# A second score row taken behind the next turns, three of ten slabs copied by VectorE, later traffic held until k is in

## What is computed

```python
def attend(q, k, v, scale):
    # query head h uses kv head h // (Hq/Hk), 128 queries at a time
    sc = jnp.einsum("bqhgd,bkhd->bhgqk", qi, k) * scale
    p = jax.nn.softmax(sc, axis=-1)
    return jnp.einsum("bhgqk,bkhe->bqhge", p, v)

o1 = attend(dq[:, :, :, 0], dk[:, :, :, 0], dv, sc)      # differential: 4 pairs of heads, values of 128
o2 = attend(dq[:, :, :, 1], dk[:, :, :, 1], dv, sc)
o_diff = rmsnorm(o1 - lam * o2, subln_g) * (1.0 - lam_init)
o_gqa = attend(gq, gk, gv, sc)                           # grouped: 8 query heads, 2 kv heads, values of 64
```

## Time and profile before

| | |
|---|---|
| time, median of 3 runs | 2223.13 us (2220.74 to 2223.78) |
| profiled execution: time, span | 2224.07 us, 2222.0 us |
| TensorE: products, weight loads | 1999.5 us (90%), 1490.4 us (67%) |
| VectorE, ScalarE, POOL | 1546.1 us (70%), 1378.3 us (62%), 938.0 us (42%) |
| mean granted clock of TensorE | 0.961 of full |
| first score row, last store of attention | 396.66 us, 929.06 us |
| a copy of a turned slab by ScalarE, L907 | 0.60 us, 240 of them |
| reduction of a score row, L940; softmax row, L900 | 1.49 us, 128 of them; 1.33 us, 128 of them |

### The profile page before, as it was taken

How to read it: one execution, slowest core, us unless ns; L and a number is a source line. 1 busy time by engine, 2 the same in 40 slices (tenths; PEclk the granted TensorE clock), 3 DMA queues, 4 the chain that set the end, 5 groups by cost and what they waited for, 6 DMA issues and landing times.

```text
span 2222.0 us, 36247 instructions
## 1 busy us (share of the span) xinstructions
PE 1999.5 (90%) x9592; PEld 1490.4 (67%) x9592; DVE 1546.1 (70%) x2158; ACT 1378.3 (62%) x2000; POOL 938.0 (42%) x869
## 2 busy tenths in 40 slices
PE   5899995688988889879989999999999999999993
PEld 2776664555555555467646888888877888888881
DVE  3752373585336743246446999999988999999995
ACT  2422121465656566522336999899878998999982
POOL 1010011651115511006453666656665666666663
PEclk7999998799999999888999999999999999999997
DMA  7464345711122121248536999799999977789967
GB/s 260 138 185 134 108 133 175 215 39 41 36 53 44 29 44 36 81 160 157 131 90 251 307 352 315 230 297 300 353 330 351 347 241 224 229 245 353 303 152 255
DMA packets 162651, 429.16 MB, mean 193 GB/s; under 512 B 26993, under 2 KB 82033, under 8 KB 137889
## 3 DMA queue, kind: packets, MB, share of 16 engines
q1 hardware_dynamic: 92818, 294.36, 36.6%
q0 software_dynamic: 60048, 116.89, 23.6%
q10 hardware_dynamic: 9712, 16.99, 2.6%
HBM read 360.83 MB, written 96.26 MB: 206 GB/s over the span
## 4 chain that ended last, share of the span: by engine, by line
PE 45%; DMA 6%; DVE 2%; issue 2%; ACT 1%; SPq 1%; ACTq 0%; POOL 0%; DVEq 0%; POOLq 0%
PE ps_d L2031 11%; PE ps_r L2014 8%; PE ps_r L2016 7%; PE ps_r L2015 7%; DMA w_experts<-in_w_exp_down 5%; PE ps_y L1937 4%; PE ps_y L2004 3%; PE ps_g L1954 2%; PE ps_d L1971 1%; PE ps_g L2038 1%; PE ps_t L1917 0%; DMA y_tiles_odd<-y_scratch 0%; DMA o_in<-o_scratch 0%; DVE x_row L1672 0%; DMA y_scratch<-e_y,e_target_index 0%
## 5 line engine op out<-in xcount | busy, mean ns | idle before, releaser
L1782 DVE TENSOR_TENSOR w_gate_up_low<-w_experts,w_gate_up_high 128x1024 fp32r<-128x1024 f32 x416 | 489.2, 1217 | 18.5 <-ACT w_gate_up_high L1551 18.4
L1551 ACT ACTIVATE w_gate_up_high<-w_experts 128x1024 fp32r x416 | 416.5, 1049 | 31.9 <-SPq L1309 16.9
L940 DVE TENSOR_REDUCE neg_max<-ps_scores 128x1 f32<-128x1280 f32 x128 | 190.2, 1489 | 232.9 <-PE ps_scores L1025 232.5
L2014 PE MATMUL ps_r<-w_gate_up_high,gatheredT_high 128*128 128x512 f32 x832 | 336.0, 404 | 3.0 <-DVE gatheredT_low L1788 2.7
L1440 POOL DMA_INDIRECT y_scratch<-e_y,e_target_index x104 | 288.6, 2775 | 108.0 <-POOL e_target_index L1436 93.5
L2016 PE MATMUL ps_r<-w_gate_up_high,gatheredT_low 128*128 128x512 f32 x832 | 326.8, 393 | 0.0
L2015 PE MATMUL ps_r<-w_gate_up_low,gatheredT_high 128*128 128x512 f32 x832 | 324.6, 390 | 0.0
L1817 DVE TENSOR_TENSOR w_down_low<-w_experts,w_down_high 128x2048 fp32r<-128x2048 f32 x103 | 236.1, 2293 | 43.9 <-ACT w_down_high L1576 43.4
L1426 POOL DMA_INDIRECT gathered<-h_scratch,e_gather_index x106 | 194.2, 1832 | 95.9 <-POOL e_gather_index L1423 90.8
L1025 PE MATMUL ps_scores<-k_high_low,q_high 128*128 128x512 f32 (+1 forms) x384 | 166.4, 433 | 58.8 <-DMA k_high_low<-k_scratch 29.5
L1576 ACT ACTIVATE w_down_high<-w_experts 128x2048 fp32r x103 | 197.9, 1922 | 32.9 <-issue 32.9
(11 more groups left out here) (278 smaller groups left out, 3937.0 us busy)
## 6 DMA issues: line engine op xcount, KB each, us to landing
w_experts<-in_w_exp_gate SPq DMA_DIRECT2D x64, 1024.0 KB, 9.5
w_experts<-in_w_exp_up SPq DMA_DIRECT2D x64, 1024.0 KB, 13.8
w_experts<-in_w_exp_down SPq DMA_DIRECT2D x64, 1024.0 KB, 17.4
w_mod_later<-in_w_mod ACTq DMA_DIRECT2D x32, 512.0 KB, 3.8
w_mod_first<-in_w_mod SPq DMA_DIRECT2D x4, 2048.0 KB, 15.5
w_in_raw<-in_w_in SPq DMA_DIRECT2D x32, 256.0 KB, 3.5
k_high_low<-k_scratch POOLq DMA_DIRECT2D x10, 640.0 KB, 8.8
values<-in_tokens SPq DMA_DIRECT2D x10, 512.0 KB, 11.3
```

The costliest lines, as they stand in the source:

```text
L1551: act.activation(split_slice(eH, j), raw_slice(ring, slot, j), ACT.Copy).then_inc(X["wH"], 1)
L1782: nc.vector.tensor_tensor(split_slice(eL, j), raw_slice(ring, slot, j), split_slice(eH, j).bitcast(F32), ALU.subtract).then_inc(X["wL"], 1)
L2014: nc.tensor.matmul(psR[:], xH[:, k], eH[:, k], start=(k == 0), stop=False)
```

## The change

Three things are edited, all in `attention`.

1. **Order on TensorE.** Score row 1 of a grouped unit u+1 was made behind the last turns of unit u-1, ahead of its last product. It is now made in unit u, behind its turn 0. Differential units keep the old order. On VectorE and ScalarE `rowmax(u+1, 1)` and `exp(u+1, 1)` stand where they stood, at the beginning of unit u.
2. **Who copies a slab.** In grouped units slabs 1, 5 and 8 are copied by VectorE, the other seven by ScalarE as before. There are two semaphores in place of one, and whoever waits for a slab waits for its own.
3. **SP's early traffic.** SP waits until all ten slabs of k are in before it issues what `tail` needs. The wait for the q of unit 1 ahead of `w_out_ahead` goes.

The first `out_p` below is ScalarE's, the second VectorE's.

```diff
+    def by_dve(g):
+        return units[g // KT_N][0] == "g" and g % KT_N in (1, 5, 8)
+
+    def wait_out(eng, g):
+        if by_dve(g):
+            eng.wait_ge(s_evd, sum(1 for h in range(g + 1) if by_dve(h)))
+        else:
+            eng.wait_ge(s_ev, sum(1 for h in range(g + 1) if not by_dve(h)))
...
             sp.dma_start(sg[:], a["subln_g"].broadcast_to([P, DIFF_V])).then_inc(s_g, 16)
+            for w in s_k:
+                sp.wait_ge(w, 32)
             sp.dma_start(rows_d, rows[0:1].rearrange("p r n -> p (r n)")).then_inc(s_later, 16)
...
             sp.dma_start(token[:], a["k_token"]).then_inc(s_later, 16)
-            sp.wait_ge(s_q[1], 64)
             sp.dma_start(wa[:], a["w_out"][0, 0:wa.shape[1] * P, :].rearrange("(k p) n -> p k n", p=P)).then_inc(s_later, 16)
...
             def out_p(u, kt):
                 g = u * KT_N + kt
+                if by_dve(g):
+                    return
...
+            def out_p(u, kt):
+                g = u * KT_N + kt
+                if not by_dve(g):
+                    return
+                dve.wait_ge(s_tr, g + 1)
+                if g >= KEEP:
+                    dve.wait_ge(s_pv, g - KEEP + 1)
+                nc.vector.tensor_copy(pd[:, g % KEEP], pT(u, kt)).then_inc(s_evd, 1)
...
                 for kt in range(KT_N):
+                    out_p(u, kt)
                     if kt in at:
                         rowmax(u + 1, at[kt])
...
+            def second_row_late(u):
+                return units[u][0] == "g"
+
             LAG = 3
             for u in range(NU):
                 at = rows_at(u)
                 for kt in range(KT_N):
                     tr(u, kt)
+                    if kt == 0 and u + 1 < NU and second_row_late(u + 1):
+                        qk(u + 1, 1)
                     if kt == 1 and u >= 1:
                         back(u - 1)
...
                         if kt == KT_N - LAG:
                             qk(u + 2, 0)
-                        if kt == KT_N - 1:
+                        if kt == KT_N - 1 and not second_row_late(u + 2):
                             qk(u + 2, 1)
                     pv(u, kt)
```

More of the change, by code:

```diff
@@ L776, in attention @@
         s_ev = b.sem(ph, "probsT_out")
+        s_evd = b.sem(ph, "probsT_out_dve")
         s_pv = b.sem(ph, "pv_done")
@@ L1031, in tr @@
                 if g is not None:
-                    pe.wait_ge(s_ev, g + 1)
+                    wait_out(pe, g)
                 for j in range(4):
@@ L1046, in pv @@
                     return
-                pe.wait_ge(s_ev, g + 1)
+                if kind == "g":
+                    wait_out(pe, g - 1)
+                wait_out(pe, g)
                 if kt < 2 and u >= 1:
```

## The result

Median 2190.6 us (2189.07 to 2195.12) against 2222.33 for the kernel before on the same chip: ratio 0.9861, 95% interval 0.9844 to 0.9878. Forecast 2190. The profiled execution took 2191.77 us (span 2190.1, granted clock 0.966).

What follows compares the result with a forecast made beforehand. TensorE, 90% busy, was taken to bound the kernel, with holes at attention's border and in grouped units. Terms 12.4 + 20.5 + 0.6 + 0.6 - 1.0 = 33.1 us gave 2191.0, about 2190 against the median; range 2181 to 2204.

Steps and rivals of the forecast that it cites:

- Start: Border into attention: with the clearing's large packets kept back, TensorE's first score row begins 12.4 us earlier (10.6 to 14.5).
- Grouped units: Twelve of 16 grouped units take 16.19 us instead of 17.90, 1.71 less each; 20.5 us in all (12 to 27).
- S+3.4: Grouped unit: turn 3 would be ready about 3.4 us after first turn S; its bank frees at S+3.95, about 0.55 wait.
- Borders: Last differential unit into each of two grouped blocks: 1.3 us later in front, 0.3 net gain each, 0.6 for both.
- the rival: Clock falls in front of grouped blocks, behind a TensorE wait of about 2.3 us: some 1.5 us per block, 2193; chance 0.08.
- Against it: the 1.66 us at the same place passed without a fall: Argument against the clock falling before grouped blocks: the old trace's 1.66 us wait there brought no fall.
- my 53.23 - 0.3: Two units around the first border: 53.23 us before, less the forecast net gain of 0.3 per border.
- priced it at 1.5: Cost of a clock fall at each grouped block: slower score row and following turn, some 1.5 us.
- Units 10, 11, 12 and 22: Seventh grouped unit's slab 5 wait shrinks 0.6 us; the eighth's next turn comes 1.0 later; last two units gain nothing named.
- clearing and q would collide: Rival: the moved clearing catches q of unit 2, TensorE waits for it, plus 4.5 us, 2194; chance 0.08.

Runs made afterwards that it cites:

- x9: Changed kernel with only the clearing of y_scratch issued at once, as before; the other early traffic stays kept back: 2208.17 us, ratio 0.9918.
- x10: Changed kernel with only the clearing of y_scratch kept back; small transfers issued at once, w_out waits for q of unit 1 again: 2198.64 us, ratio 0.9877.
- x3: Changed kernel without VectorE's copies: ScalarE copies all ten slabs, late score row and kept-back traffic stay: 2220.81 us, ratio 0.998.
- x4: Changed kernel with the second score row in its old place; VectorE's copies and kept-back traffic stay: 2200.84 us, ratio 0.9894.
- x2: Changed kernel with SP's early traffic put back where it was; order and copies stay: 2205.01 us, ratio 0.9909.
- x1: Kernel before with the kept-back traffic alone, order and copies as before: 2213.66 us, ratio 0.9954.
- x5: Changed kernel with the second score row in its old place in front of grouped blocks (units 3 and 15), late only inside them: 2183.2 us, ratio 0.9806.
- x6: x5 with slabs 5 and 8 of unit 11 copied by ScalarE again: 2186.86 us, ratio 0.9827.
- x12: x5 with the late score row behind the second turn inside grouped blocks, and VectorE copying slab 2 there too: 2195.64 us, ratio 0.9879.
- x7: Changed kernel with slab 1 of units 3 and 15 copied by VectorE too: 2189.49 us, ratio 0.983.
- x8: Changed kernel with 16 useless turns ahead of the wait for the mix in units 3 and 15: 2191.77 us, ratio 0.9846.
- x11: Changed kernel with x7's VectorE copies and x8's useless turns together: 2187.34 us, ratio 0.9834.

## Why the forecast was right, term by term

**Start: right.** Forecast 12.4, measured 12.12 in the wait (29.46 to 17.34). x9 and x10 show that the clearing makes 11.0 of it. The other 1.5 us of the first row's 13.6 came from the stage ahead: SP issues `sub_gain` at 370.64, where the same issue stood about 1.5 us later before. The change doesn't touch that stage, so this part is luck. The Trainium skill (DMA: Bandwidth & Descriptors, section Queues, rings and completion order) says that an engine takes turns between queues by whole packets. The trace agrees: from 376 to 386 in x9, while the clearing ran, each queue got 48 packets, the clearing's with 3.15 MB and those of k and q with 0.25 MB.

**Grouped units: right.** Forecast 1.71 a unit and 0.55 us at turn 3, measured 1.81 and 0.46; 20.4 in all for 20.5. That the total fits so well is luck in part: ten units gave 1.81 each, but units 4 and 16, whose wait at turn 3 is 0.87 and not 0.46, gave 1.16 each. The rows also put turn 3 ready a little later than the S+3.4 that I wrote; it was ready at S+3.55. x3 and x4 show that the whole gain needs both parts: a plain grouped unit gives 0.46 us with the order alone, 0.98 with the copies alone and 1.81 with both.

**Borders: the walk right, the rival true all the same.** I gave +0.6 for both, they cost 4.0. The step that failed is "Against it: the 1.66 us at the same place passed without a fall". Where the clock stayed, in unit 15 of x9, the two units take 27.87 + 24.93 = 52.80 us, which is my 53.23 - 0.3 within 0.13. The fall puts up to 2.7 us on that, where I priced it at 1.5. The wait for the mix is 1.85 us, where I had 2.3. I also carried turn 2 only as 1.3 us later, and not as a second idle stretch behind the first; it is 2.65 us long in unit 15 of x9.

What the runs say of that clock: with the late row at the border and nothing repaired (the changed kernel, x2, x3, x9, x10) the clock fell to the 1.2 GHz level in 9 of 10 passes. In the old order (before, x1, x4, x5, x6, x12) it fell in none of 12; with one wait repaired (x7, x8) in 3 of 4; with both (x11) in none of 2. The less idle time, the fewer falls, which speaks for the idle time as the cause; the two passes of x11 are few to show it. It doesn't settle each case: x9 passed twice through the same instructions and fell once, and x3 fell behind its 1.80 us at turn 3 in two of ten plain grouped units. The Trainium skill (TensorE: Matmul & The Clock Gate, section Why this matters for your kernels) says to leave no long idle gaps between bursts of matmuls. The gaps that it has in mind are longer than the ones here, so by it the clock should have stayed; the measurements say otherwise.

**Units 10, 11, 12 and 22.** Unit 11 cost 1.06 for 1.0. Unit 10 gave 1.6 for 0.6: I carried only its wait for slab 5 and cancelled the rest. Unit 12's 0.9 I did not have. It is the fall of the earlier trace rows that no longer happens, and x6 shows one such trade: unit 11 a microsecond shorter, unit 12 a microsecond longer at a lower clock. It is no rule. Where unit 11 took 25.36 the clock fell in unit 12 in three of four executions (before, x1, x6, but not x3); where VectorE copied its slabs 5 and 8, in two of ten (x4 and x7). Why it falls in one and not in another stays open.

So 4.6 us lost at the borders met 4.4 that I had not counted on: the stage ahead 1.5, unit 0 0.9, unit 10 1.0, unit 12 0.9 and unit 22 0.5, less 0.3 at the start and 0.1 in the grouped units. The total was hit by luck, more closely than its terms deserve. That clearing and q would collide did not happen: no wait for q stands in the changed trace.

**Left open.** From the start of the first turn of the gathered tokens to the start of the last product of `w_down_high` with `e_actT_high` the experts took 990.0 to 1000.3 us in the fourteen profiled executions, with the same code and no order by the change (before 991.4, changed 994.8, x1 996.3, x2 1000.3). Differences of 3 to 5 us between totals, as between x5 and x6, can't be laid on attention. The stage between the last copy of attention and that first turn took 251.8 to 255.2 us in twelve executions, and 258.3 and 259.4 in x9 and x10, which issue SP's early traffic in another order; whether that is the cause was not tried.

## What to carry to other kernels

Keep large-packet fills out of a window in which another engine waits for small-packet loads: one clearing cost 11 us. A reordering and a change of who copies can be a loss and a gain when taken alone, and more than their sum together: price each alone, since here the order lost 8.6 us by itself and gained 5.0 on top of the copies. Where a reordering takes the filler out of a wait, price the granted clock behind it too, and leave the old order at the edges of a block (x5, 7 us in four units).

## What was not expected of the hardware

The granted clock is not settled by the instructions alone: the same instructions, behind the same first wait of 1.85 us, took 24.93 us in one unit and 27.64 in another of one execution (x9). And a wait that is shortened can lose its own gain one unit later, if the clock then falls (25.36 + 27.32 us in x6 against 26.42 + 26.21 in x5); it did not in x3 (25.36 + 26.22).
